# First attention of a two-layer kernel: the causal mask moves from TensorE products to GpSimd edits of the running sums

## What is computed

```
log_f = log_sigmoid(f_logit + b_f)
cum = cumsum(log_f, axis=1)                      # one running sum per head and row
for blk in range(L // Q_BLOCK):                  # 8 blocks of 128 queries
    q0 = blk * Q_BLOCK; kend = q0 + Q_BLOCK
    s = (q[q0:kend] . k[:kend]) * scale
    s = s + cum[q0:kend, None] - cum[None, :kend]
    s = where(k_pos <= q_pos, s, NEG_INF)        # only the block's own 128 keys are affected
    p = softmax(s); out = p . v[:kend]
```

## Time and profile before

| | us |
|---|---|
| median of 3 runs | 3589.28 (3587.01 to 3590.35) |
| the profiled execution, its own time | 3586.24 |
| its span in the profile | 3584.4 |
| TensorE busy | 3479.1 (97%) |
| VectorE, ScalarE, GpSimd busy | 1387.6, 941.1, 967.8 |

### The profile page before, as it was taken

How to read it: one execution, slowest core, us unless ns; L and a number is a source line. 1 busy time by engine, 2 the same in 40 slices (tenths; PEclk the granted TensorE clock), 3 DMA queues, 4 the chain that set the end, 5 groups by cost and what they waited for, 6 DMA issues and landing times.

```text
span 3584.4 us, 44185 instructions
## 1 busy us (share of the span) xinstructions
PE 3479.1 (97%) x17275; PEld 2873.2 (80%) x17275; DVE 1387.6 (39%) x2452; ACT 941.1 (26%) x1575; POOL 967.8 (27%) x421
## 2 busy tenths in 40 slices
PE   7899999999999999999999999998999999999999
PEld 6688877888877888888778888887788888888887
DVE  6883443123335333333643444335124312232234
ACT  4223434322242111111433333332322211111112
POOL 1552102232215333333212222221322132222321
PEclk9999999999999999999999999999999999999999
DMA  4233012212312111111221212213123111111111
GB/s 131 62 76 95 22 54 65 70 53 65 123 53 83 47 48 56 48 47 47 71 86 47 66 53 59 78 42 115 53 65 111 36 60 52 47 47 47 47 47 59
DMA packets 203976, 226.83 MB, mean 63 GB/s; under 512 B 19224, under 2 KB 177604, under 8 KB 203340
## 3 DMA queue, kind: packets, MB, share of 16 engines
q1 hardware_dynamic: 178556, 169.85, 15.4%
q10 hardware_dynamic: 20912, 44.54, 3.6%
q0 software_dynamic: 4384, 10.74, 0.9%
HBM read 191.30 MB, written 31.69 MB: 62 GB/s over the span
## 4 chain that ended last, share of the span: by engine, by line
PE 87%; DVE 4%; issue 4%; ACT 2%; POOL 1%; DMA 1%; ACTq 0%; DVEq 0%; POOLq 0%
PE ps L274 18%; PE ps L319 16%; PE ps L301 13%; PE ps L302 13%; PE ps L295 13%; PE ps L770 4%; PE ps L2838 2%; PE ps L2809 1%; POOL wlo L266 1%; PE ps L2826 1%; PE ps L2321 1%; PE ps L336 1%; PE ps L510 1%; ACT whi L258 1%; PE ps L2302 1%
## 5 line engine op out<-in xcount | busy, mean ns | idle before, releaser
L266 POOL TENSOR_TENSOR wlo<-raw,whi 128x2048 fp32r<-128x2048 f32 (+1 forms) x162 | 699.4, 4318 | 1731.1 <-ACT whi L258 1730.2
L301 PE MATMUL ps<-h_lo,whi 128*128 128x512 f32 x1856 | 723.8, 390 | 2.0 <-POOL wlo L266 2.0
L302 PE MATMUL ps<-h_hi,wlo 128*128 128x512 f32 x1856 | 723.5, 390 | 0.0
L258 ACT ACTIVATE whi<-raw 128x2048 fp32r<-128x2048 f32 (+1 forms) x162 | 288.1, 1779 | 883.1 <-PE ps L295 595.9
L295 PE MATMUL ps<-h_hi,whi 128*128 128x512 f32 x1856 | 461.6, 391 | 5.0 <-issue 2.7
L295 PEld LDWEIGHTS ps<-h_hi,whi 128*128 128x128 f32 x1856 | 349.2, 188 | 79.0 <-issue 5.8
L301 PEld LDWEIGHTS ps<-h_lo,whi 128*128 128x128 f32 x1856 | 349.5, 188 | 75.7 <-POOL wlo L266 3.1
L302 PEld LDWEIGHTS ps<-h_hi,wlo 128*128 128x128 f32 x1856 | 349.3, 188 | 72.6
L1157 DVE TENSOR_TENSOR big<-big,ps 128x512 f32<-128x512 f32 x400 | 274.4, 687 | 240.3 <-PE ps L274 240.2
L319 PE MATMUL ps<-h_lo,whi 128*128 128x512 f32 x880 | 352.2, 400 | 2.0 <-POOL wlo L266 1.9
L319 PE MATMUL ps<-h_hi,wlo 128*128 128x512 f32 x880 | 344.8, 392 | 0.0
(11 more groups left out here) (335 smaller groups left out, 4817.8 us busy)
## 6 DMA issues: line engine op xcount, KB each, us to landing
raw<-in_w_ff_dram SPq DMA_DIRECT2D x32, 1024.0 KB, 5.2
raw<-in_w_in_dram SPq DMA_DIRECT2D x57, 512.0 KB, 4.6
raw<-in_w_in_dram SPq DMA_DIRECT2D x28, 1024.0 KB, 5.3
raw<-in_w_ffn_gate_dram SPq DMA_DIRECT2D x11, 1024.0 KB, 5.3
raw<-in_w_ffn_up_dram SPq DMA_DIRECT2D x11, 1024.0 KB, 5.3
raw<-in_w_ffn_down_dram SPq DMA_DIRECT2D x11, 1024.0 KB, 4.9
yt<-y_keep ACTq DMA_DIRECT2D x20, 512.0 KB, 3.9
raw<-in_w_out_dram SPq DMA_DIRECT2D x8, 1024.0 KB, 5.0
```

What stands on the lines that cost most here:

```text
L258: nc.scalar.activation(whi[c % 2][:, 0:cols], raw[c % 2][:, 0:cols], ACT.Copy).then_inc(s_hi.sem, 1)
L266: nc.gpsimd.tensor_tensor(wlo[c % 2][:, 0:cols], raw[c % 2][:, 0:cols], whi[c % 2][:, 0:cols].bitcast(F32), ALU.subtract).then_inc(s_lo.se ...
L301: nc.tensor.matmul(ps[:, bank + n, :], w(0, k, m * P, P), src[1][:, k, sl], start=False, stop=False)
L302: last = nc.tensor.matmul(ps[:, bank + n, :], w(1, k, m * P, P), src[0][:, k, sl], start=False, stop=k == ks - 1)
```

## The change

The products with the mask go, and so do the two ScalarE copies that made `mask_a`. Instead GpSimd edits `CK` in place, 128 sums of both heads at a time: before a block is looked at, `masked` keeps a copy of its own 128 sums in `own` (two buffers), then subtracts the mask (0 or a large negative number for each query and key) from them; after both `least` of the block, `plain` copies the kept sums back, since later blocks see these keys without a mask. The last block of a pair is not put back: the next pair's load overwrites it. `least` of head 0 now also waits until its block's sums are masked and the block's before are put back. The calls of `split_lo` that GpSimd made in one go are now placed between these steps.

```diff
-                nc.scalar.activation(mask_a[:, 0, :], ident, ACT.Copy)
-                nc.scalar.activation(mask_a[:, 1, :], m_causal, ACT.Copy, scale=-1.0).then_inc(mask_made.sem, 1)
...
             def pool(self, e):
-                for k in range(1, 5):
+                for k in range(1, 3):
                     split_lo(e, unit_no(self.u + k))
+
+                def masked(n):
+
+                    p, b = n // 8, n % 8
+                    at = CK[:, :, b * P:(b + 1) * P]
+                    if b == 0:
+                        e.wait_ge(d_in.sem, self.c[0] + 16 * (p + 1))
+                    if b == 4:
+                        e.wait_ge(d_in2.sem, self.c[1] + 16 * (p + 1))
+                    if n >= 2:
+
+                        e.wait_ge(sums_plain.sem, self.sp_ + 7 * ((n - 2) // 8) + min((n - 2) % 8, 6) + 1)
+                    nc.gpsimd.tensor_copy(own[:, n % 2], at).then_inc(sums_step.sem, 1)
+                    e.wait_ge(sums_step.sem, self.ss + n + 1)
+                    nc.gpsimd.tensor_tensor(at, at, m_causal.unsqueeze(1).to_broadcast([P, 2, P]), ALU.subtract
+                                            ).then_inc(sums_masked.sem, 1)
+
+                def plain(n):
+
+                    e.wait_ge(maxima.sem, self.m + 2 * n + 2)
+                    nc.gpsimd.tensor_copy(CK[:, :, n % 8 * P:(n % 8 + 1) * P], own[:, n % 2]).then_inc(sums_plain.sem, 1)
+                masked(0)
                 for p in range(self.N):
-                    if p % 2:
-                        split_lo(e, unit_no(self.u + (0, 5, 0, 6)[p]))
+                    for b in range(8):
+                        if 8 * p + b + 1 < 8 * self.N:
+                            masked(8 * p + b + 1)
+                        if b < 7:
+                            plain(8 * p + b)
+                        k = {(0, 0): 3, (0, 6): 4, (1, 4): 5, (3, 2): 6}.get((p, b))
+                        if k is not None:
+                            split_lo(e, unit_no(self.u + k))
                     e.wait_ge(rows_out.sem, self.o + 8 * (p + 1))
                     e.dma_start(scratch["y_keep"][2, :, p, :], Yc[:, p % 2, :]).then_inc(d_ay[p % 2].sem, 16)
...
-                    if b == 0 and h == 0:
-                        e.wait_ge(d_in.sem, self.c[0] + 16 * (p + 1))
-                    if b == 4 and h == 0:
-                        e.wait_ge(d_in2.sem, self.c[1] + 16 * (p + 1))
+                    if h == 0:
+                        e.wait_ge(sums_masked.sem, self.sm + 8 * p + b + 1)
+                        if 7 * p + b:
+                            e.wait_ge(sums_plain.sem, self.sp_ + 7 * p + b)
...
-                        if own:
-                            for h in range(2):
-                                last = nc.tensor.matmul(o[h][:, w - P:w], mask_a[:, 0, :], mask_a[:, 1, :], start=False, stop=True)
+                            last = nc.tensor.matmul(o[h], QG[d[h], p % 2, q], KF[d[h], p % 2, k], start=False, stop=True)
+                            if lo + w == kend:
                                 last.then_inc(scores.sem, 1)
```

More of the change, by code:

```diff
@@ L158, in hybrid_kernel @@
         rope = phase([("below_rope", [P, HIGH], F32), ("rope", [P, 2, L], F32)])[1]
-        (QF, QG, KF, KG, VT, PB, PT, CK, Yc, RD, RS, mask_a, mn, dn) = phase([
+        (QF, QG, KF, KG, VT, PB, PT, CK, Yc, RD, RS, own, mn, dn) = phase([
             ("QF", [P, 2, L], F32R), ("QG", [P, 2, L], F32R), ("KF", [P, 2, L], F32R), ("KG", [P, 2, L], F32R),
@@ L163, in hybrid_kernel @@
             ("CK", [P, 2, L], F32), ("Yc", [P, 2, L], F32), ("RD", [P, 2, 2, HD], F32), ("RS", [P, P], F32),
-            ("mask_a", [P, 2, P], F32R), ("mn", [P, 2, 2], F32), ("dn", [P, 2, 2], F32)])
+            ("own", [P, 2, 2, P], F32), ("mn", [P, 2, 2], F32), ("dn", [P, 2, 2], F32)])
         at_big = ExitStack()
@@ L222, in hybrid_kernel @@
         rot, q_loaded = sig("rotation_step"), sig("q_weights_loaded")
+        sums_masked, sums_plain, sums_step = sig("running_sums_masked"), sig("running_sums_plain"), sig("running_sums_kept")
         d_dil = [sig(f"pass_stored{j}") for j in range(2)]
@@ L358, in first_tiles @@
             tiles(1, KT - 1)
-        compute_signals = [qk_ready, v_ready, v_turned, rotated, q_hi, q_lo, v_feat, v_taken, scores, maxima, probs, p_turned, p_taken,
+        compute_signals = [sums_masked, sums_plain, sums_step, qk_ready, v_ready, v_turned, rotated, q_hi, q_lo, v_feat, v_taken, scores, maxima, probs, p_turned, p_taken,
                            values, rows_out, mask_made, gv_ready, gv_taken, pair_loaded, pair_step, pair_exp, ct_turned, ct_taken, inverted, scale_rows, scale_taken, rot, rope_step, rope_act, pe_a, pe_b, dve_a, dve_b, act_a, dv, ac, po, pe_s, d_in, d_in2, d_tab, d_gain, *x_pair,
@@ L2014, in __init__ @@
                 self.iv, self.sr, self.st = inverted.take(8 * n), scale_rows.take(8 * n), scale_taken.take(8 * n)
-                self.mk, self.ql = mask_made.take(1), q_loaded.take(16 * n)
+                self.ql = q_loaded.take(16 * n)
+                self.sm, self.sp_, self.ss = sums_masked.take(8 * n), sums_plain.take(7 * n), sums_step.take(8 * n)
                 self.c = d_in.take(16 * n), d_in2.take(16 * n)
@@ L2272, in score @@
                     else:
-                        e.wait_ge(mask_made.sem, self.mk + 1)
                         e.wait_ge(q_lo.sem, self.l + 4)
@@ L2278, in score @@
                         w = min(HALF, kend - lo)
-                        k, own = slice(lo, lo + w), lo + w == kend
+                        k = slice(lo, lo + w)
                         o = [ps[:, 2 * h + lo // HALF, 0:w] for h in range(2)]
@@ L2285, in score @@
                         for h in range(2):
-                            last = nc.tensor.matmul(o[h], QG[d[h], p % 2, q], KF[d[h], p % 2, k], start=False, stop=not own)
-                        if own:
-                            for h in range(2):
-                                last = nc.tensor.matmul(o[h][:, w - P:w], mask_a[:, 0, :], mask_a[:, 1, :], start=False, stop=True)
+                            last = nc.tensor.matmul(o[h], QG[d[h], p % 2, q], KF[d[h], p % 2, k], start=False, stop=True)
+                            if lo + w == kend:
                                 last.then_inc(scores.sem, 1)
```

## The result

The kernel after takes **3601.49 us** in the median of 8 runs (3599.78 to 3605.15); the kernel before, timed beside it, 3588.82 us (8 runs). The ratio is 1.0035, 95% interval 1.0026 to 1.0045: slower by 12.7 us. The profiled execution took 3601.63 us, its span 3599.7, against 3586.24 and 3584.4: 15.3 us more in the spans.

A forecast was written before the change was run, and what follows sets the result against it. TensorE, busy 97% of the span, was taken to bound the kernel. Saving -6.4, stalls with pair changes +16.9 and clock +4.5 gave +15.0 us: 3589.28 us becomes 3604 us, range 3593 to 3611.

The forecast's parts named there:

- all four stalls: Attention stage: TensorE waits where a GpSimd split is queued ahead of `masked`; 16.5 us together; likeliest case, 73%.
- saving: Attention stage, TensorE: 23 of 32 pairs of mask products count, at 0.28 us each; 6.4 us saved, bounds 6 and 9.
- stall (0, 0): Pair 0, block 0: `least` of (0, 2) waits behind split, `masked` and `plain`; TensorE loses 3.5 us.
- stall (0, 6): Pair 0, block 6: `least` of (1, 0) waits behind the split and `masked`; TensorE loses 3.5 us.
- stall (1, 4): Pair 1, block 4: `least` of (1, 6) waits behind the split and GpSimd's steps; TensorE loses 2.2 us.
- stall (3, 2): Pair 3, block 2: `least` of (3, 4) is late with no fill left to cover it; TensorE loses 7.3 us.
- pair changes: At (1, 7) and (2, 7), `masked` stands between landing sums and `least`; 0 to 1 us each, 0.4 in all.
- clock: TensorE's granted clock drops after long waits: 2 + 1.5 + 1 = 4.5 us lost, bounds 1.5 and 7.
- GpSimd's steps: GpSimd: copy 0.45 us, subtraction 0.7, 0.08 between dependent instructions; `masked` about 1.3, with `plain` 1.9 us.
- Rival 1: Waits of pairs 0 and 1 vanish in the fills, only (3, 2) stalls: +3.3 us, or 3593 us; 14%.
- Rival 2: GpSimd and VectorE hold each other up, new steps take twice as long: +22 us, or 3611 us; 8%.
- Rival 3: New steps never reach the path, slack before `least` suffices: -6.4 to -9.0 us, 3583 to 3580 us; 5%.

The follow-up runs named there:

- products left out: Kernel before without the 64 mask products, no mask applied at all and no new GpSimd steps: 3582.10 us, ratio 0.9981 to the kernel before.
- (1, 4) split late: Kernel after with only the split of (1, 4) moved, to (1, 5): 3598.65 us, ratio 1.0030 to the kernel before.
- last split late: Kernel after with only the split of (3, 2) moved, to (3, 6): 3590.84 us, ratio 1.0005 to the kernel before.
- all splits late: Kernel after with the four splits moved to (0, 1), (0, 7), (1, 5) and (3, 6): 3582.78 us, ratio 0.9982 to the kernel before.
- wait filled: Kernel after with 28 unread 512-column products added on TensorE at step (3, 3) ahead of `value`: 3599.69 us, ratio 1.0034 to the kernel before.
- (0, 0) split late: Kernel after with only the split of (0, 0) moved, to (0, 1): 3599.06 us, ratio 1.0031 to the kernel before.
- (0, 6) split late: Kernel after with only the split of (0, 6) moved, to (0, 7): 3596.61 us, ratio 1.0022 to the kernel before.
- last split one step late: Kernel after with the splits moved to (0, 1), (0, 7), (1, 5) and (3, 3): 3585.41 us, ratio 0.9993 to the kernel before.

## Why the prediction was right

Forecast were 3604 us, range 3593 to 3611, and 0.78 for slower; measured 3601.49. The likeliest case is the one that came, all four stalls, at the four places and through the chain worked out. In the profile it looks as the last part said, with waits of 2.80, 3.27, 1.57 and 7.63 us for 3.3, 3.4, 2 and 8. The profile's 15.3 us is nearer to the 15.0 forecast than the working deserves, as the table shows. Its terms, with the stalls and the clock taken apart by the `Yc` times (a stall is measured where the clock stayed full, or by the wait itself):

| term | predicted | measured | from |
|---|---|---|---|
| saving | -6.4 | -5.3 | products left out, stage end |
| stall (0, 0) | 3.5 | 3.0 | (0, 0) to (0, 2): 13.97 with the (1, 4) split late, clock full; 11.01 without the stall |
| stall (0, 6) | 3.5 | 3.5 | (0, 6) to (0, 7): 10.87 with the last split late, clock full; 7.39 without the stall |
| stall (1, 4) | 2.2 | 2.1 | (1, 4) to (1, 5): 12.60; 10.47 without |
| stall (3, 2) | 7.3 | 7.0 | wait 7.63 less 0.63 |
| pair changes | 0.4 | 0.8 | below |
| clock | 4.5 | 5.8 in this execution | what is left of +16.9 at (3, 7) |
| sum | +15.0 | +16.9, of which 15.3 at the end of the span | |

**Luck in the sum.** The terms' errors add up to +1.9 (saving 1.1 less, stalls 0.9 less, pair changes 0.4 more, clock 1.3 more); 1.6 us then came back in stages that the change does not touch, for reasons that the sum did not hold.

**The saving** was mis-sized in its working, though by little in sum: the pair is worth 0.24 us, not the 0.28 of the earlier trace rows, and counts at some 20 steps, not 23. The chain's pieces pointed to the right kind of step, but the first steps of a pair give nothing more often than they suggest, and four steps that were left out, (2, 3) and (3, 3) to (3, 5), do give theirs.

**GpSimd's steps.** Copy 0.39 to 0.42 (0.45 predicted), subtraction 0.72 to 0.75 (0.7), `masked` with `plain` from 557.24 to 558.78, 1.5 us (1.9). The interpolation from the earlier trace rows held for the two-input operation. The hand-over was put too long: the copy behind the subtraction starts 0.67 us after it (557.71 to 558.38), where 0.7 and 0.08 were reckoned. The stalls are shorter than predicted by 0.9 us together. The Trainium skill, "GPSIMD Engine Reference", section 4.1, compares with VectorE: two-input operations about twice as slow on GpSimd, one-input ones roughly line-rate. The trace agrees for the copy, 0.40 us where VectorE's copy of 256 elements out of PSUM took 0.42; for two inputs the nearest pair, GpSimd's subtraction and VectorE's `least` of 256 elements, which took 0.42, is not the same operation and gives a factor of 1.7.

**The pair changes.** With all splits late, the shift at (1, 7) is 0.22 later than at (1, 6) where it is 0.23 earlier with the products left out, and at (2, 7) 0.10 later than at (2, 6) where it is 0.24 earlier: 0.45 and 0.34, 0.8 us together, within the 0 to 2 given, and no wait over 1 us. This is most of the 1.0 us that all 92 instructions cost.

**The clock** was right in its kind, and its sizes are the middle of what executions show. What the low clock cost behind each wait (us, the intervals between `Yc` against 13.97 and 10.87, and the stretch from the fourth wait to the next stage against 23.07):

| profile of | (0, 0) | (0, 6) | (3, 2) |
|---|---|---|---|
| kernel after | 1.1 | 2.2 | 2.65 |
| last split late | 1.0 | 0.0 | |
| wait filled | 0.0 | 1.6 | |
| (0, 0) split late | | 2.2 | 1.3 |
| (0, 6) split late | 2.2 | | 2.1 |
| (1, 4) split late | 0.0 | 1.6 | 1.8 |
| mean | 0.9 | 1.5 | 2.0 |
| predicted | 1 | 1.5 | 2 |

(1, 4) cost nothing, as said. That the means come so near is luck in part: for (3, 2) the prediction took the low clock of the earlier trace rows to last 3.5 us from 2448.70, but a mean of 0.56 over 2452 to 2454 puts its end near 2453.8, 5 us behind, which by the same reckoning is 2.5 us and not 1.7. The kernel after's own profile has high ones, 5.9 in all, against the 5.8 left over in the table above.

**The 15.3 of the profiles and the 12.7 of the medians.** The kernel after's profiled execution lies at its median (3601.63 against 3601.49); the kernel before's lies 2.6 us below its own (3586.24 against 3588.82). So the 2.6 us stand on the side of the kernel before, and where that execution gained them is not shown. The terms without the clock give +11.1, with the mean clock +15.5; the interval of the medians, 9.3 to 16.2 us, holds both.

**The rivals.** Rival 1, only (3, 2) stalls: with the last split moved, the three others still cost 8.1 us (3590.84 less 3582.78), and each has its wait in the profile. Rival 2, the engines hold each other up: GpSimd's steps took 0.39 to 0.42 and 0.72 to 0.75 whatever VectorE did, the splits 4.49 to 4.59, VectorE was busy for 1387.8 us where it was 1387.6 before, and with the same steps beside the same VectorE work the run with all splits late is within 1.0 us of the one without steps. The rule of the Trainium skill, "SBUF — State Buffer", section "SBUF: two separate sides", that the two engines share a port pair, could have cost at most what is in that microsecond here. Rival 3, slack enough: true of the late splits, and its 3583 to 3580 is what that kernel measures, 3582.78; not true of the places that the change chose.

## What to carry to other kernels

Moving work from a full engine to one that is 9% busy gains only if the new work's place in that engine's in-order queue is free when it is wanted: look at the longest item there, and put it behind the short steps that the critical engine is soon to need, not ahead. Here one number for each of four splits turned +12.7 us into -6.1 us with the same instructions. Work out the stall as (long item + steps behind it), from the time at which the long item can start, less the time until the bound engine needs the result: for the four places here that gave 3.5, 3.5, 2.2 and 7.3 us for 3.0, 3.5, 2.1 and 7.0 measured, and 2.7 for 3.0 with the last split one step late; and count a saved pair of matmuls only where the bound engine itself sets the step.

## What the runs showed of the hardware

The granted clock after a wait near 3 us is not settled by the wait's length. In `Merge`, the kernel after waited 3.24 us (product at 612.42) and went on at 1.00; the run with the last split one step late waited 3.15 us and went on at half rate for over 6 us:

```profile
595.27 0.80 PE L302 MATMUL ps<-y_lo,whi 128*128 128x512 f32 x1 [3.15 <-POOL wlo L267]
```

```profile
596.00:598.00 2.00, 2.00 (x7) 1.54 (x5) 0.00 (x0) 1.63 (x3) 1.78 (x1) 0.50 0.77 249
598.00:600.00 2.00, 2.00 (x6) 1.63 (x5) 0.69 (x1) 0.00 (x0) 2.00 (x1) 0.50 0.08 21
600.00:602.00 2.00, 2.00 (x7) 1.54 (x7) 0.00 (x0) 0.00 (x0) 0.78 (x1) 0.64 0.09 9
```

From there to the next wait, near 966 us, that run took 373.91 us and the kernel before 371.06: 2.9 us lost in a stage that no edit touched. This and the low clock behind its stall are why that run's profile lies 7.6 us over the one with all splits late (4.6 of it at the next stage's start) and its median only 2.6. A shorter wait at the same place can be followed by a drop too: with the products left out it was 2.51 us, where the kernel before went on at full clock after 2.88 (1.00 over 595 to 599).

```profile
590.00:593.00 3.00, 3.00 (x8) 2.33 (x8) 0.00 (x0) 1.98 (x3) 2.42 (x1) 0.50 0.57 171
```

After the waits of 1.57 us no drop was seen; after those of 7.4 to 7.6 us, in five profiles, always one, and in the four of them that can be compared it cost between 1.3 and 2.7 us. What decides between 2.5 and 3.3 us stays open. For a difference of a few us, one profile is too few, and a wait near 3 us is worth up to 2.9 us more than its length.
